# The begin of each layer in a two-layer encoder kernel: another order of the first products, smaller first loads, the first low weights on VectorE

## The reference

```
proj = x @ w_in[i]
glu_in, gates, z, xbc, dt_raw = split(proj, ...)
...
dt_f = softplus(dt_raw[..., :32] + dt_bias[0])
dt_b = softplus(dt_raw[..., 32:] + dt_bias[1])
...   # conformer branch, bidirectional Mamba-2 scan on z, xbc, dt (8 groups, chunks of 128)
h  = LayerNorm(alpha * x + merged @ w_o)
h2 = LayerNorm(alpha * h + SwiGLU(h))
x  = h2 + RMSNorm(p[i] @ w_ple) * sigmoid(h2 @ w_ple_gate)
```

## Time and profile before

| what | us |
|---|---|
| median of 3 runs (lowest, highest) | 2387.91 (2387.74, 2389.31) |
| the profiled execution | 2392.21 |
| its span in the profile | 2390.6 |
| PE busy (share) | 2348.7 (98%) |
| DVE busy | 1515.9 (63%) |
| ACT busy | 1359.1 (57%) |
| POOL busy | 593.7 (25%) |
| DMA, mean rate over the span | 168 GB/s read |

### The profile page before, as it was taken

How to read it: one execution, slowest core, us unless ns; L and a number is a source line. 1 busy time by engine, 2 the same in 40 slices (tenths; PEclk the granted TensorE clock), 3 DMA queues, 4 the chain that set the end, 5 groups by cost and what they waited for, 6 DMA issues and landing times.

```text
span 2390.6 us, 35334 instructions
## 1 busy us (share of the span) xinstructions
PE 2348.7 (98%) x11436; PEld 1940.3 (81%) x11436; DVE 1515.9 (63%) x2567; ACT 1359.1 (57%) x2238; POOL 593.7 (25%) x721
## 2 busy tenths in 40 slices
PE   8999999999999999999999999999999999999999
PEld 6878788887878788888788787888878778888886
DVE  5899999999645311113768999999995461111147
ACT  5756657466564554344657566664755655543446
POOL 3423324243111111111124143432421111111110
PEclk9999999999999999999999999999999999999999
DMA  7677575857889688898665866857678787888985
GB/s 204 141 158 160 115 178 114 185 123 159 179 184 211 158 194 192 194 207 188 165 153 117 182 131 151 178 112 165 136 163 187 171 198 173 193 191 197 210 188 139
DMA packets 112261, 402.90 MB, mean 169 GB/s; under 512 B 12400, under 2 KB 12400, under 8 KB 112112
## 3 DMA queue, kind: packets, MB, share of 16 engines
q0 software_dynamic: 54144, 195.06, 48.8%
q1 hardware_dynamic: 55728, 200.56, 25.4%
q10 hardware_dynamic: 2240, 5.42, 0.6%
HBM read 398.89 MB, written 2.10 MB: 168 GB/s over the span
## 4 chain that ended last, share of the span: by engine, by line
PE 89%; DVE 5%; ACT 2%; issue 2%; DMA 2%; POOL 0%; ACTq 0%; SPq 0%; POOLq 0%; DVEq 0%
PE bank L879 24%; PE bank L881 24%; PE bank L880 24%; PE bank L921 3%; PE bank L922 3%; PE bank L924 2%; PE bank L995 2%; PE bank L1001 1%; PE bank L983 1%; DMA w_lo<-w_stream 1%; PE bank L1210 1%; DVE tmp_m L1392 1%; PE bank L966 1%; PE bank L951 1%; PE bank L1012 1%
## 5 line engine op out<-in xcount | busy, mean ns | idle before, releaser
L356 POOL DMA_DIRECT2D w_lo<-w_stream x376 | 328.6, 874 | 1565.5 <-ACT w_lo L470 1510.1
L879 PE MATMUL bank<-x_hi,w_hi 128*128 128x512 f32 x1728 | 686.2, 397 | 1.5 <-DMA w_lo<-w_stream 1.5
L881 PE MATMUL bank<-x_hi,w_lo 128*128 128x512 f32 x1728 | 673.4, 390 | 0.0
L880 PE MATMUL bank<-x_lo,w_hi 128*128 128x512 f32 x1728 | 672.8, 389 | 0.0
L469 ACT ACTIVATE w_hi<-w_raw 128x1024 fp32r<-128x1024 f32 (+1 forms) x378 | 399.7, 1057 | 280.2 <-PE bank L881 250.1
L470 ACT ACTIVATE w_lo<-w_raw 128x1024 fp32r<-128x1024 f32 (+1 forms) x378 | 396.8, 1050 | 0.0
L879 PEld LDWEIGHTS bank<-x_hi,w_hi 128*128 128x128 f32 x1728 | 324.6, 188 | 70.8 <-issue 5.1
L881 PEld LDWEIGHTS bank<-x_hi,w_lo 128*128 128x128 f32 x1728 | 324.4, 188 | 68.9
L880 PEld LDWEIGHTS bank<-x_lo,w_hi 128*128 128x128 f32 x1728 | 324.7, 188 | 67.8 <-issue 3.2
L1305 DVE SCALAR_TENSOR_TENSOR z_a<-glu_out,params,z_a 128x497 f32<-128x497 f32 (+14 forms) x480 | 324.0, 751 | 0.0
L1763 DVE TENSOR_TENSOR glu_out<-bank,sigmoids 128x512 f32<-128x512 f32 x44 | 30.5, 692 | 404.3 <-PE bank L881 404.3
(11 more groups left out here) (250 smaller groups left out, 3610.0 us busy)
## 6 DMA issues: line engine op xcount, KB each, us to landing
w_raw<-w_stream SPq DMA_DIRECT2D x362, 512.0 KB, 5.0
w_lo<-w_stream POOLq DMA_DIRECT2D x360, 512.0 KB, 7.5
w_raw<-w_stream SPq DMA_DIRECT2D x16, 384.0 KB, 3.7
w_lo<-w_stream POOLq DMA_DIRECT2D x16, 384.0 KB, 6.0
z_b<-x_in SPq DMA_DIRECT2D x4, 512.0 KB, 7.6
out<-z_b SPq DMA_DIRECT2D x4, 512.0 KB, 6.2
ple_p<-p_in ACTq DMA_DIRECT2D x2, 512.0 KB, 5.9
w_ple_in<-w_ple ACTq DMA_DIRECT2D x2, 512.0 KB, 11.3
```

What stands on the lines that cost most here:

```text
L356: gp.dma_start(wlo[:, s, 0:n], w_stream[cyc, s, :, 0:n].bitcast(F32R), accum_op=ALU.add).then_inc(lo_done[s], 16)
L879: pe.matmul(dst, wh, mh, start=first, stop=False)
L880: pe.matmul(dst, wh, ml, start=False, stop=False)
L881: return pe.matmul(dst, wl, mh, start=False, stop=last)
```

## The change

- **Step products the other way round.** `step_products` replaces the 24 wide matmuls, ACT's copy and the transposes: for each 128 tokens, `x` is stationary (128x128) and the step weights stream, 128 columns (high and low weights side by side in `w_dt_split`) by the high `x`, and 64 columns by the low `x`. That is 4 x 8 x 2 = 64 matmuls; the result has tokens on partitions, in two halves that DVE adds (one operation more). They stand behind slot 0's `dense`, not ahead of it.
- **Slot 0 as `x` comes.** The first 24 matmuls of a layer are slot 0's `dense`, three for each `x` tile.
- **Loads.** The first two `x` tiles come alone (256 KB each), the others in pairs; raw weight tile 0 is queued behind the first.
- **First low weights.** In the first layer DVE makes the low parts of slots 0, 1 and 2 by subtraction from the raw tile; POOL issues no accumulating DMA for them. SP waits for that subtraction (`start_lo`) before it overwrites a raw buffer. In the second layer POOL issues them as before, but now waits until they have landed and tells PE by `start_lo`.
- **Waits.** ACT and DVE do not wait for POOL's constants before their first work.
- **`z_b` not zeroed.** The first pair's output is copied to `z_b`, not added.
- **TensorE warmed.** 14 float32 matmuls of 128 columns on the `ones` constant, into bank 7, at the program's start.
- ACT's `hi` of slot 2 moves ahead of the exponent table's use.

```diff
+X_TILES = {0: 1, 1: 1, 2: 2, 4: 2, 6: 2}
+BY_VECTOR = 3
+WARM = 14
...
-            for m in range(0, KT, 2):
-                sp.dma_start(zb[:, m:m + 2, :], x_in[:, m:m + 2, :]).then_inc(x_loaded[m // 2], 16)
+            for i, (m, n) in enumerate(X_TILES.items()):
+                sp.dma_start(zb[:, m:m + n, :], x_in[:, m:m + n, :]).then_inc(x_loaded[i], 16)
...
+            sp.wait_ge(start_lo[0], seen(1))
             tile(0, 2)
+            sp.wait_ge(start_lo[1], seen(1))
             tile(0, 3)
+            sp.wait_ge(start_lo[2], seen(1))
...
-            with gp.Fori(0, LAYERS) as L:
+            for L in range(LAYERS):
                 base = L * CYCLES
-                lo(base, 0, 1, 2, 3)
-
-                gp.wait_ge(xl_done, seen(NORMS * KT * L + KT))
-                settle(gp)
-                gp.memset(zb[:, :, :], 0.0).then_inc(zb_zero, 1)
+                for slots in ((0, 1), (2,)) if L else ():
+                    lo(base, *slots)
+                    for s in slots:
+                        gp.wait_ge(lo_done[s], 16 * base)
+                        gp.sem_inc(start_lo[s], 1)
+                lo(base, 3)
...
-                act.wait_ge(dt_done, seen(2 * L + 1))
-                act.activation(sg[0:2 * HEADS, :], bank[4][0:2 * HEADS, :], ACT.Copy).then_inc(dt_evac, 1)
...
+            def step_products():
+                for c in range(CH):
+                    t, dst = slice(c * P, (c + 1) * P), quarters(bank[6])[:, c, :]
+                    for k in range(KT):
+                        w = slice(k * 2 * HEADS, (k + 1) * 2 * HEADS)
+                        def of_high(first, last):
+                            return pe.matmul(dst.rearrange("p (x e) -> p x e", x=2), xh[:, k, t], dw[:, :, w], start=first, stop=last)
+                        if k < KT - 1:
+                            of_high(k == 0, False)
+                        pe.matmul(dst[:, 0:2 * HEADS], xl[:, k, t], dw[:, 0, w], start=False, stop=False)
+                    q = of_high(False, True)
                 q.then_inc(dt_done, 1)
...
+            pe.wait_ge(consts, 1)
+            for _ in range(WARM):
+                pe.matmul(bank[7][:, 0:P], ones[:, :], ones[:, :], start=True, stop=True)
...
-                pe.wait_ge(dtw_lo, seen(L + 1))
                 for k in range(KT):
                     pe.wait_ge(xl_done, seen(NORMS * KT * L + k + 1))
-                    w = slice(k * 2 * HEADS, (k + 1) * 2 * HEADS)
-                    q = three(bank[4][0:2 * HEADS, :], dwh[:, w], dwl[:, w], xh[:, k, :], xl[:, k, :], k == 0, k == KT - 1)
-                q.then_inc(dt_done, 1)
+                    dense(base, 0, xh, xl, ks=(k,), layer=L)
+                pe.wait_ge(dtw_lo, seen(L + 1))
+                step_products()
...
-            dve.wait_ge(consts, CONSTS)
+            def first_low(s):
+                dve.wait_ge(hi_done[s], seen(1))
+                dve.tensor_tensor(wlo[:, s, :], raw[:, s % 2, :], whi[:, s, :].bitcast(F32),
+                                  ALU.subtract).then_inc(start_lo[s], 1)
...
+                step(dve.tensor_tensor(biased, sums[:, 0], bias.unsqueeze(2).broadcast_to([P, 2, CH, HEADS]), ALU.add))
+                dve.wait_ge(dve_order, issued())
+                dve.tensor_tensor(biased, biased, sums[:, 1], ALU.add).then_inc(dt_v, 1)
...
+                        if j == 0:
+                            r = dve.tensor_copy(zb[:, m, :], bank[s][:, :])
+                        else:
+                            r = dve.tensor_tensor(zb[:, m, :], zb[:, m, :], bank[s][:, :], ALU.add)
```

More of the change, by code:

```diff
@@ L213, in build @@
         evac = [sem(f"evac{s}") for s in range(SLOTS)]
+        start_lo = [sem(f"start_lo{s}") for s in range(BY_VECTOR)]
         consts = sem("consts")
-        x_loaded = [sem(f"x_loaded{m}") for m in range(KT // 2)]
+        x_loaded = [sem(f"x_loaded{m}") for m in X_TILES]
         par_loaded = sem("par_loaded")
@@ L348, in _ @@
         def _(gp):
-            open_(gp, rhs_ready, rms_done, zb_zero)
+            open_(gp, rhs_ready, rms_done)
             def lo(cyc, *slots, n=WT):
@@ L682, in _, with first_hi @@
             act.wait_ge(dtw_loaded, 16)
-            act.activation(dwh[:, :], tmf, ACT.Copy).then_inc(dtw_hi, 1)
-            act.wait_ge(consts, CONSTS)
-            for m in range(KT):
-                if m % 2 == 0:
-                    act.wait_ge(x_loaded[m // 2], 16)
-                act.activation(xh[:, m, :], zb[:, m, :], ACT.Copy).then_inc(xh_done, 1)
-                if m == 1:
-                    hi((0, 0), 0)
-            hi((0, 0), 1)
+            act.activation(dw[:, 0, :], tmf, ACT.Copy).then_inc(dtw_hi, 1)
+            def first_hi(s):
+                act.wait_ge(raw_ready[s], 16)
+                act.activation(whi[:, s, :], raw[:, s % 2, :], ACT.Copy).then_inc(hi_done[s], 1)
+            for m in range(KT):
+                if m in X_TILES:
+                    act.wait_ge(x_loaded[list(X_TILES).index(m)], 16)
+                act.activation(xh[:, m, :], zb[:, m, :], ACT.Copy).then_inc(xh_done, 1)
+                if m == 0:
+                    first_hi(0)
+            first_hi(1)
+            act.wait_ge(consts, CONSTS)
             settle(act)
@@ L881, in three, with weights_ready, slot_ready, dense @@
                 return pe.matmul(dst, wl, mh, start=False, stop=last)
-            def slot_ready(cyc, s):
-                pe.wait_ge(lo_done[s], 16 * (cyc[0] + 1))
+            def weights_ready(cyc, s, layer=None):
+                if layer is None or s >= BY_VECTOR:
+                    pe.wait_ge(lo_done[s], 16 * cyc[0] + (16 if s >= BY_VECTOR else 0))
+                else:
+                    pe.wait_ge(start_lo[s], seen(layer + 1))
+            def slot_ready(cyc, s, layer=None):
+                weights_ready(cyc, s, layer)
                 pe.wait_ge(evac[s], seen(cyc[1]))
-            def dense(cyc, s, mh, ml, nk=KT, ks=None):
+            def dense(cyc, s, mh, ml, nk=KT, ks=None, layer=None):
                 ks = ks or range(nk)
                 if ks[0] == 0:
-                    slot_ready(cyc, s)
+                    slot_ready(cyc, s, layer)
                 for k in ks:
@@ L902, in projection @@
                 if ks[0] == 0:
-                    pe.wait_ge(lo_done[s], 16 * (cyc[0] + 1))
+                    weights_ready(cyc, s)
                     pe.wait_ge(evac[b], seen(cyc[1] + m // SLOTS))
@@ L1103, in pair @@
                 low, high = range(KT // 2), range(KT // 2, KT)
-                if first:
-                    dense(c0, 0, xh, xl, ks=low)
-                    steps_transpose(L)
-                    dense(c0, 0, xh, xl, ks=high)
-                else:
+                if not first:
                     dense(c0, 0, xh, xl)
-                dense(c0, 1, xh, xl)
-                dense(c0, 2, xh, xl)
+                dense(c0, 1, xh, xl, layer=L if first else None)
+                dense(c0, 2, xh, xl, layer=L if first else None)
                 if first:
@@ L1580, in _ @@
                 rest_of_x(0, m)
+                if m == 0:
+                    first_low(0)
+            for s in range(1, BY_VECTOR):
+                first_low(s)
+            dve.wait_ge(consts, CONSTS)
             restart()
@@ L1689, in add_mamba @@
                         dve.wait_ge(used[s], seen(c0 + c + 1))
-                        dve.tensor_tensor(zb[:, m, :], zb[:, m, :], bank[s][:, :], ALU.add).then_inc(evac[s], 1)
+                        if j == 0:
+                            r = dve.tensor_copy(zb[:, m, :], bank[s][:, :])
+                        else:
+                            r = dve.tensor_tensor(zb[:, m, :], zb[:, m, :], bank[s][:, :], ALU.add)
+                        r.then_inc(evac[s], 1)
                     dve.wait_ge(evac[0], seen(c0 + 4))
@@ L1816, in _ @@
                 dve.wait_ge(dtw_hi, seen(L + 2))
[L1817 removed]
+                rest(dw[:, 1, :], tmf, dw[:, 0, :], dtw_lo)
                 dve.wait_ge(estd_ready, seen(L + 1))
```

27 lines of the change are left out of this document (8 added, 19 removed).

## The result

The changed kernel is slower: 2397.58 us (median of 7 runs, 2393.14 to 2402.00) against 2389.31 us for the kernel before, timed beside it (7 runs), ratio 1.0028 with a 95% interval of 1.0018 to 1.0039. I had forecast 2385.0 and a range that ended at 2391.0. Measured once more, beside the experiments, the same kernel again came out slower, ratio 1.0035 (1.0021 to 1.0049).

A forecast was written before the change was run, and what follows sets the result against it. PE, busy for 98% of the span, was taken as a stream of matmuls. First layer -3.6 and second +0.7 sum to -2.9 us, from the median 2387.91 to 2385.0; range 2381.8 to 2391.0.

The forecast's parts named there:

- (a), (b): First layer: first weight tile lands at 7.65, PE starts at 10.0; slot 0's 24 matmuls at 0.23 us end at 15.5.
- Rival 2: First layer: warming ends by about 7.6, PE stands 2.4 us, clock is low at 10.0; costs 2.0 us, 2387.0; chance 0.17.
- (c): First layer, step products: 64 narrow matmuls at 0.105 us each take 6.7 us (between 5.8 and 7.7), to 22.2.
- (d): First layer, slots 1 and 2: 48 matmuls at 0.23 us take 11.1 us, to 33.3, with their weights ready in time.
- Rival 4: Step products: narrow ones are cheaper, at 0.08 us each layer gains 1.6 more, 2381.8; chance 0.10.
- Rival 5: Step products: fp32r loses its rate on few columns, 64 take 13.4 us, 6.7 more per layer, +10.5, 2398.4; chance 0.05.
- (e): First layer, cumulative sums at 33.3 instead of 36.91; without the memset DVE's chain takes 10.1 us, 0.8 ahead of PE.
- Rival 6: DVE's step chain: memset gone but the stall stays, PE waits 2.9 us in each layer, +2.9, 2390.8; chance 0.04.
- (f): First layer, z_tiles starts at 41.2 instead of 44.77, gain 3.6 us; slot 1's accumulating DMA taken at 7.5 us to landing.
- rival 3: The raw load for slot 1's next tile stays slow (8.0 us) in both layers: +3.1 us, 2391.0; chance 0.12.
- (h), second layer: Warming, removed waits and smaller loads' extra issue at nothing; second layer's PE work to the sums 23.3 us, loss 0.7.
- (g): Each layer's first pair: a copy in place of eight additions saves at most 2.1 us of DVE's time; taken as nothing.

The follow-up runs named there:

- woven_128: The changed kernel with the step products woven into slot 0 (8 after each 3 wide matmuls), each streaming 128 columns; 2392.19 us, ratio to before 1.0010.
- columns_128: The changed kernel with each of the 64 step products streaming 128 columns, where 32 of them streamed 64; 2390.67 us, ratio to before 1.0007.
- old_products: The changed kernel with the 24 wide step products, ACT's copy and the transposes back; 2389.36 us, ratio to before 0.9988; measured again 2390.27 us, 1.0002.
- experiment 10: old_products with the zeroing of z_b on GpSimd put back (the result still copied, not added); 2397.16 us, ratio to before 1.0032.
- nowarm: The changed kernel without its 28 warming matmuls (WARM = 0); 2397.97 us, ratio to before 1.0033.
- woven kernel: The changed kernel with the 64 narrow step products woven into slot 0, eight after each three wide matmuls; 2396.85 us, ratio to before 1.0029.

## Why the prediction was wrong, step by step

**(a), (b) right.** PE starts slot 0 at 9.80 (forecast 10.0) and ends it at 15.38 (15.5). Rival 2 is out: the warming began only at 3.72, when its constants were there, and so ended at 9.97 and not at 7.6, with no stand behind it. I had its length right and its place wrong, to the kernel's good. Whether the stand of 2.4 us that it feared would have cost the clock was not run. Behind 2.0 us (woven_128, after the warming) and 3.0 us (columns_128, second layer) PE went on at full pace, behind 3.3 us (old_products, experiment 2) at half pace.

**(c) is the step that failed.** It priced all 64 products from short rows at the full clock, and had nothing for a loss of that clock inside the stream. At the full clock a product is 0.111 us: 7.1 us for 64, against 6.7, which is a small miss. In the first layer the 64 took 9.3 us (15.38 to 24.70). The low clock went on into slots 1 and 2, **(d)**, which I had at 0.23 us a matmul throughout: 13.6 us (24.70 to 38.25) where columns_128 took 11.0 (23.11 to 34.10) for the same work. That is 2.2 + 2.6 = 4.8 us. In the second layer 8.1 and 13.1 us, 1.0 + 2.1 = 3.1 us. Together 7.9 at the two begins.

At the full clock the Trainium skill's pace ("TensorE: Matmul & The Clock Gate", back-to-back issue gap, about 81 ns at 128 columns) isn't reached in this fp32r stream either: 0.111 us for 128 columns. Rival 4 is out.

Rival 5 had the right place and size, "dearer, straight in PE's stream, it decides from 0.128 us each" (here it came to 0.146 in the first layer and 0.127 in the second), but for a wrong reason, and so with too small a chance, and it stopped at the last product. I had considered the clock only where PE stands still.

The kernel before had a warning in it. Its granted clock dips four times in the pairs of groups, and each costs 1.7 us. Three of these dips come at matmuls of the very kind that gave the price of 0.105: PE does eight passes of 64 columns, stands for some 1.45 us and does eight more (from 281.11, 424.08 and 1608.80), and the clock falls 1 to 2 us after these begin:

```profile
281.11 1.08 PE L995 MATMUL bank<-x_tok,decay 128*128 128x64 f32 x8 [1.45 <-DVE tmp_y L1416]
```

```profile
283.00:285.00 2.00, 2.00 (x6) 1.58 (x5) 1.90 (x5) 0.51 (x2) 0.00 (x0) 0.50 1.09 244
```

The fourth follows a stand of 1.9 us among wide matmuls. So these rows don't tell the narrow passes from the stand, and at five other such places in the same execution there is no dip; but the granted clock behind them would have given rival 5 its reason.

A second account agrees on the time lost to the clock. Taking (1 - granted clock) x 10 us over all full stretches of 10 us, the kernel before loses 6.8 us and the changed one 15.3. The difference, 8.5, is made of 5.1 at 20 to 40 and 3.4 at 1210 to 1220. Single dips in the pairs (each 1.7 us) are in all kernels and equal in number in these two, four; some come at the same place in most of the kernels (one between 280 and 290), others don't.

**(e) right:** the tensor_scalar takes 0.40 instead of 4.00, the chain 10.0 where I had said 10.1, and it isn't waited for. Rival 6 is out, and experiment 10 shows the stall to cost PE 7.4 us of waiting as soon as PE is early.

**(f) too high.** Where the clock holds, columns_128 starts z_tiles at 42.34 and old_products at 42.39, a gain of 2.4 and not 3.6. PE was ready earlier and waited:

```profile
42.39 0.36 PE L940 MATMUL bank<-w_hi,x_hi 128*128 128x256 f32 x1 [1.46 <-issue]
```

The profile says "issue", but an accumulating DMA for slot 0 of the next cycle was issued at 32.6 and took 9.7 us to land, which ends at 42.3; that it was this landing that PE waited for is inferred from the times. When the kernel was run again it was issued at 32.4, took 9.2, and PE began at 41.69. I had taken 7.5, the median of all such transfers, for slot 1's and had not looked at slot 0's. The raw load that rival 3 spoke of took 8.3 to 8.9 us in old_products; that part of the rival is true in the first layer.

**(h), second layer, too low.** columns_128 has its sums at 1223.07, 0.6 us ahead of before, though it had been 2.8 ahead in the first layer. Its lead lasted to the end of the first layer (2.7 us). It lost 1.1 in front of the second, where PE stood still for 3.0 us (before 1.9), as its list of waits from 40 to 1200 us shows, and 1.0 in it (23.64 us from the first matmul to the sums, before 22.62):

```profile
PE bank L888 <- DVE x_lo L1459: 3.0, 1, 3.0
```

I had granted the second layer's work 0.7, and the stand ahead of it nothing, since x was there before. But where something else than PE's own work ends a wait, a kernel that comes earlier only waits longer.

**Sum.** Without the fall I had -2.9. columns_128 has +0.2 us by its medians (1.7 by its ratio, 1.0007) and -1.6 by its span in one profile, with one dip of the clock fewer; so 1.3 to 3.1 us of the gain were not there, and up to 4.6 by the ratio. The fall itself is 6.4 us by the medians on one chip (2397.06 against 2390.67). With -2.9 + 3.1 + 6.4 = 6.6 the two together make the 6.7 us of the measured ratio.

The traces give less than the medians. Of the 7.9 us that the changed kernel loses at the two begins, most of the first layer's part is taken up again before the second: its sums start 4.1 us behind those of columns_128, but the second layer only 0.3 (1199.73 against 1199.43), since PE stands for 0.8 us in front of it and not for 3.0. What is lost in the second layer lasts longer: 3.5 us at the sums and 2.5 at the end of the span (2391.5 against 2389.0), and in the second profile of the changed kernel 5.1 and 4.4. Both are profiles of the fastest execution of their series; how the others come to more wasn't seen.

**(g) as assumed.** PE's waits behind DVE in the pairs are no shorter with the copies than with the additions; this row answers to the first of the earlier trace rows:

```profile
PE bank L1011 <- DVE tmp_y L1437: 11.1, 8, 1.5
```

**Left open.** What ends PE's stand in front of the second layer (0.8 to 3.3 us in these kernels): no matching DMA of weights was found; x_lo, which the list names, isn't the tile that PE needs first. Whether nowarm's 2.8 us at the begin reach its end. What about the 64-column products lets the clock fall is not known beyond the streams that were run: a stream of them alone, or 64 and 128 columns by turns in another proportion, wasn't tried. How the woven kernel's executions of over 2400 us look wasn't seen.

## What to carry to other kernels

In a stream of fp32r matmuls that each load new 128x128 weights, 64 and 128 columns cost the same here (0.111 us), so price the columns before you save them. Such a stream with 64 columns in every second matmul was busy without a gap and still lost the clock, which the same stream with 128 in all did not, and the slow pace then hit the wide matmuls behind it. Read the granted clock by stretches around every stream of a new kind. And an engine that stalls unseen, as DVE did under the memset, becomes a bound on the day that the engine in front of it gets faster, so take the stall out with the speed-up. Last, time lost or won at one place need not reach the end: compare the stands behind it as well.

## What the hardware showed that I had not expected

- Clock and busy time part: 0.50 granted with PE busy for 4.71 of 4.71 us, in a stream of 128- and 64-column matmuls by turns; 1.00 throughout in the streams of 128 columns, of 128 columns twice as long, and of 256.
- The pace of a product is the same for 64 and 128 columns (0.111 us) and 0.12 for 256.
- After the fall, wide matmuls ran at 0.43 us until about 30 (from 24.70), more than 5 us, before 0.23 came back.
- From a cold begin, slot 0's wide matmuls ran at half pace for about 6 us (10.34 to 16.4 in nowarm) before full pace came, and 14 small float32 matmuls (28 passes, 6.25 us) ahead of them were enough to avoid that.
- Accumulating DMAs of 512 KB took 9.0 to 9.8 us to land at 30 to 42 us of the program, against a median of 7.5.
